# A two-block network on one core: the order of work around the first attention, and the row maxima of the second

## What is computed

```python
# first block
s = jnp.einsum('bqhd,bkhd->bhqk', qb, k) * scale
s = s + cqb[..., :, None] - c_bhs[..., None, :]
s = jnp.where(causal, s, -jnp.inf)
p = jax.nn.softmax(s, axis=-1)                      # 8 heads of 64, 1024 keys
sgu = spatial_gating(jax.nn.gelu(z), ...)           # layer norm, 8 groups of 128x128
merged = concatenate([rms_norm(attn), rms_norm(sgu)])
x = x + merged @ w_out
...
# second block: 16 query heads, window of 128 plus 256 context keys, and a sink
logits = concatenate([s_lat, s_ctx, sink])
p = jax.nn.softmax(logits)
```

## Time and profile before

| | us |
|---|---|
| median of 3 runs (2851.93 to 2857.03) | 2852.97 |
| the profiled execution | 2850.02 |
| its span, first to last instruction | 2848.2 |
| PE busy | 2735.5 (96% of the span) |
| DVE busy | 2040.7 (72%) |
| ACT busy | 1312.3 (46%) |

### The profile page before, as it was taken

How to read it: one execution, slowest core, us unless ns; L and a number is a source line. 1 busy time by engine, 2 the same in 40 slices (tenths; PEclk the granted TensorE clock), 3 DMA queues, 4 the chain that set the end, 5 groups by cost and what they waited for, 6 DMA issues and landing times.

```text
span 2848.2 us, 35308 instructions
## 1 busy us (share of the span) xinstructions
PE 2735.5 (96%) x13692; PEld 2189.3 (77%) x13692; DVE 2040.7 (72%) x2919; ACT 1312.3 (46%) x2019; POOL 555.6 (20%) x499
## 2 busy tenths in 40 slices
PE   7999999999999999999999999999999399999996
PEld 6777778788778888988888876666788288888885
DVE  5344444888885688887867656766765689999997
ACT  4344533433323455433222345444323277777775
POOL 0011011655555110511111121111100300010000
PEclk9999999999999999999999999999999699999998
DMA  4210113344661998233222261111664599999996
GB/s 147 54 45 30 45 50 133 99 141 138 188 181 57 350 296 238 81 93 115 89 72 77 104 197 33 41 42 38 207 215 156 222 352 398 396 395 397 396 395 236
DMA packets 270618, 494.12 MB, mean 173 GB/s; under 512 B 30124, under 2 KB 141892, under 8 KB 269940
## 3 DMA queue, kind: packets, MB, share of 16 engines
q1 hardware_dynamic: 240864, 396.40, 40.0%
q0 software_dynamic: 29440, 95.43, 10.4%
q10 hardware_dynamic: 148, 0.04, 0.0%
HBM read 424.60 MB, written 67.21 MB: 173 GB/s over the span
## 4 chain that ended last, share of the span: by engine, by line
PE 88%; DVE 7%; ACT 2%; issue 2%; DMA 1%; POOL 1%; POOLq 0%; DVEq 0%; SPq 0%; ACTq 0%
PE PS L132 82%; PE PS L135 6%; DVE m L141 3%; ACT m L138 1%; DVE m L150 1%; DVE m L147 1%; DMA m<-h_scratch 1%; POOL m L141 1%; DVE m L183 0%; DVE m L186 0%; DVE m L180 0%; ACT L138 0%; DVE m L156 0%; DVE small L144 0%; DMA m<-in_x_dram 0%
## 5 line engine op out<-in xcount | busy, mean ns | idle before, releaser
L132 PE MATMUL PS<-m,m 128*128 128x512 f32 (+6 forms) x11818 | 2532.7, 388 | 22.5 <-DVE m L141 9.8
L132 PEld LDWEIGHTS PS<-m,m 128*128 128x128 f32 (+2 forms) x11818 | 1985.8, 184 | 501.5 <-issue 94.3
L138 ACT ACTIVATE m<-m 128x512 fp32r<-128x512 f32 (+5 forms) x893 | 811.5, 929 | 898.7 <-PE PS L132 386.7
L141 DVE TENSOR_TENSOR m<-m,m 128x512 fp32r<-128x512 f32 (+5 forms) x920 | 1024.7, 1143 | 219.3 <-ACT m L138 197.2
L138 ACT ACTIVATE m<-PS 128x512 f32<-128x512 f32 (+3 forms) x481 | 268.3, 581 | 500.6 <-PE PS L135 310.5
L141 DVE TENSOR_TENSOR m<-PS,m 128x512 f32<-128x512 f32 (+1 forms) x456 | 300.6, 685 | 191.7 <-PE PS L132 143.8
L141 POOL TENSOR_TENSOR m<-m,m 128x512 f32<-128x512 f32 (+4 forms) x176 | 273.2, 1557 | 604.1 <-DVE m L141 259.9
L135 PE MATMUL PS<-ident,m 128*128 128x128 f32 x1650 | 231.4, 279 | 67.2 <-DVE m L156 36.0
L135 PEld LDWEIGHTS PS<-ident,m 128*128 128x128 f32 x1650 | 192.3, 143 | 114.9 <-DVE m L156 36.3
L150 DVE CUSTOM_DVE_ANT_0 m<-PS,m 128x640 f32<-128x640 f32 (+4 forms) x192 | 146.3, 774 | 97.1 <-PE PS L132 97.1
L138 ACT ACTIVATE m<-m,small 128x640 f32<-128x640 f32 (+4 forms) x200 | 157.4, 790 | 73.4 <-DVE small L150 66.7
(11 more groups left out here) (88 smaller groups left out, 483.6 us busy)
## 6 DMA issues: line engine op xcount, KB each, us to landing
m<-in_w_exp_gate_dram SPq DMA_DIRECT2D x64, 1024.0 KB, 8.7
m<-in_w_exp_up_dram SPq DMA_DIRECT2D x64, 1024.0 KB, 9.0
m<-in_w_exp_down_dram SPq DMA_DIRECT2D x64, 1024.0 KB, 8.6
m<-in_w_mod_dram SPq DMA_DIRECT2D x48, 512.0 KB, 3.8
m<-in_w_gate_up_dram SPq DMA_DIRECT2D x44, 512.0 KB, 6.4
m<-in_w_in_dram SPq DMA_DIRECT2D x21, 1024.0 KB, 5.2
m<-in_w_in_dram SPq DMA_DIRECT2D x25, 512.0 KB, 5.2
x_scratch<-m POOLq DMA_DIRECT2D x24, 512.0 KB, 3.9
```

Of the source, the lines that this page charges most:

```text
L132: return Unsent() if self.e is None else self.e.matmul(o, l, r, start=first, stop=last, **k)
L138: return Unsent() if self.e is None else self.e.activation(o, i, fn, **k)
L141: return Unsent() if self.e is None else self.e.tensor_tensor(o, a, b, op)
```

## The change

It has four parts, and no transfer of SyncE or GpSimd is added or taken away.

1. **First attention.** In step 0 the first filler call stands ahead of the scores of step 1; in all other steps it stands behind the first two transposes, so that the twelve filler matmuls form one run.
2. **z.** The rounding of `W_Z + 2` moves ahead of the squares of the tiles that `o1_scale(7)` writes (ACT) and ahead of `o1_scale(7)` (DVE). ACT takes the four GELUs out of PSUM first, then all eight high parts of `at8`, then `W_Z + 3`, then the four GELUs in SBUF.
3. **Merge.** The transposes of `zu` go in pairs between groups of `w_out`; the rounding of `W_O + 1` moves ahead of the squares.
4. **Second attention.** The reduction works on negated scores, takes the minimum and starts from the negated sink, so that `nms` comes out of it; the small instruction goes (128 of them), and the exponential has scale -1. The copy of bank 7 (16 of them) moves from DVE to ACT, behind the exponentials of the step, the last one behind `sink_exp(15)`.

```diff
@@ attn1_pe
+                if s == 0:
+                    between1(pe, 0, 0)
                 if s + 1 < NS1:
                     qk1(pe, s + 1)
                 if s:
                     values1(pe, s - 1)
-                between1(pe, s, 0)
                 for c in range(min(n, 2)):
                     turn1(pe, s, c)
+                if s:
+                    between1(pe, s, 0)
                 between1(pe, s, 2)
@@ z_act
+                if h:
+                    w_high(act, W_Z + 2)
...
-            for i in range(4):
-                act.wait_ge(*q1_out(16 + i))
-                act.activation(zv[:, i, :], zv[:, i, :], ACT.Gelu)...
-            w_high(act, W_Z + 2)
...
+            w_high(act, W_Z + 3)
+            for i in range(4):
+                act.wait_ge(*q1_out(16 + i))
+                act.activation(zv[:, i, :], zv[:, i, :], ACT.Gelu)...
@@ z_dve
+            w_low(dve, W_Z + 2)
             o1_scale(dve, 7)
@@ merge_pe
+            for i in range(5):
+                wo_group(0, 0, i)
+            pe.kept = range(6)
+            turn_zu(0)
+            turn_zu(1)
+            wo_group(0, 0, 5)
+            turn_zu(2)
+            turn_zu(3)
+            wo_group(0, 1, 0)
+            turn_zu(4)
+            turn_zu(5)
+            wo_group(0, 1, 1)
+            turn_zu(6)
+            turn_zu(7)
@@ max2
-                                         scale=0.125, scalar=-3.0e38, op0=ALU.add, op1=ALU.max, accum_out=m1)...
-                dve.wait_ge("s2_max", s, a)
-                dve.tensor_scalar(nms[:, i % 2, h:h + 1], m1, sinkr[:, h:h + 1], -1.0, ALU.max, ALU.mult)...
+                                         scale=-0.125, scalar=nsink[:, h:h + 1], op0=ALU.add, op1=ALU.min,
+                                         accum_out=nms[:, i % 2, h:h + 1])...
@@ mix_act
+                if s > 4 and s % 4 == 1:
+                    o2_take(act, s // 4 - 1)
                 for h, k in y_parts(s):
                     y_high(act, h, k)
             sink_exp(act, 15)
+            o2_take(act, 15)
@@ o2_normed
-            dve.wait_ge("o2_acc", g)
-            dve.tensor_copy(on[g % 2], PS[:, 7, :]).then_inc(*dve.did("o2_taken", g))
```

More of the change, by code:

```diff
@@ L1057, in z_act @@
                 act.activation(ma[0][:, :, tile128(i)], turned("at_turned", i), ACT.Copy).then_inc(*act.did("at_high", i))
-                if i == 1:
-                    w_high(act, W_Z + 3)
+            w_high(act, W_Z + 3)
+            for i in range(4):
+                act.wait_ge(*q1_out(16 + i))
+                act.activation(zv[:, i, :], zv[:, i, :], ACT.Gelu).then_inc(*act.did("z_out", 0, i))
             root_of(act, zr, "ln")
@@ L1091, in z_dve @@
                                   ALU.subtract).then_inc(*dve.did("at_low", i))
-                if i == 1:
-                    w_low(dve, W_Z + 3)
-            for i in range(4, 8):
+            w_low(dve, W_Z + 3)
+            for i in (4, 5, 6, 7, 0, 1, 2, 3):
                 z_norm(dve, i)
@@ L1128, in merge_sp @@
                 w_load(sp, n)
-        WO_ORDER = [(0, 0, 6), (0, 0, 7)] + [(0, 1, i) for i in range(NT)] + [
+        WO_ORDER = [(0, 1, 2), (0, 0, 6), (0, 0, 7)] + [(0, 1, i) for i in range(3, NT)] + [
             (1, kg, i) for i0 in (0, 4) for kg in range(2) for i in range(i0, i0 + 4)]
@@ L1145, in merge_pe, with wo_group, turn_zu @@
                 pe.matmul(PS[:, b, :], wsT[:, g, :], zv[:, :, g * 64:(g + 1) * 64], True, True).then_inc(*pe.did("sg_acc", g))
[L1146 to L1150, removed]
+            def wo_group(c, kg, i):
+                pe.wait_ge(*(("zu_low", i) if kg else ("at_low", i)))
+                tok_group(pe, W_O + 2 * c + kg, i, 4 * kg, 4, 8, mlhs, "wo_acc", (c, kg, i), ("x1_half", c, i))
+            def turn_zu(i):
                 pe.wait_ge(*zu_scaled(i))
                 turn4(pe, zu[:, i, :], 0, 4, "zu_turned", (i,), ("zu_low", i))
+            for i in range(5):
[12 more added lines that the diff above has]
+            turn_zu(7)
             pe.kept = ()
             for c, kg, i in WO_ORDER:
-                pe.wait_ge(*(("zu_low", i) if kg else ("at_low", i)))
-                tok_group(pe, W_O + 2 * c + kg, i, 4 * kg, 4, 8, mlhs, "wo_acc", (c, kg, i), ("x1_half", c, i))
+                wo_group(c, kg, i)
                 if (c, kg, i) == (1, 0, 7):
@@ L1164, in merge_act @@
         def merge_act(act):
+            w_high(act, W_O + 1)
             act.wait_ge("sg_out", 7)
@@ L1206, in merge_dve @@
                                          ALU.add, ALU.mult).then_inc(*dve.did("sg_out", g))
+            w_low(dve, W_O + 1)
             for h in range(2):
@@ L1214, in merge_dve @@
                 dve.tensor_scalar(zu[:, i, :], zu[:, i, :], rs8[:, i:i + 1], None, ALU.mult).then_inc(*dve.did("zu_scaled_v", i))
-            w_low(dve, W_O + 1)
             for i in range(NT):
@@ L3127, in exp2 @@
             h = heads[a]
-            act.wait_ge("s2_shift", s, a)
+            act.wait_ge("s2_max", s, a)
             v = S2[s % 3][a][:, 0:128 * len(keys2(i))]
-            act.activation(v, v, ACT.Exp, bias=nms[:, i % 2, h:h + 1], accum_out=rsum[:, i % 2, h:h + 1]).then_inc(
+            act.activation(v, v, ACT.Exp, bias=nms[:, i % 2, h:h + 1], scale=-1.0, accum_out=rsum[:, i % 2, h:h + 1]).then_inc(
                 *act.did("s2_exp", s, a))
@@ L3136, in sink_exp, with o2_take @@
             act.activation(esk[:, hs], esk[:, hs], ACT.Exp).then_inc(*act.did("sink_exp", g))
+        def o2_take(act, g):
+            act.wait_ge("o2_acc", g)
+            if g >= 2:
+                act.wait_ge("o2_out", g - 2)
+            act.activation(on[g % 2], PS[:, 7, :], ACT.Copy).then_inc(*act.did("o2_taken", g))
         def mix_act(act):
```

16 lines of the change are left out of this document (4 added, 12 removed).

## The result

The changed kernel takes 2833.54 us (median of 4 runs, 2832.55 to 2836.8), the kernel before 2852.45 beside it (4 runs). The ratio is 0.9938 [0.9926, 0.995]: faster by 18.9 us between the medians, by the interval 0.5 to 0.7%. The profiled execution took 2833.19, which is 16.8 less than the profiled execution of before (2850.02).

What follows compares the result with a forecast made beforehand. TensorE, busy 96% of the span, was taken as the bound; gains of 2.6 + 1.6 + 2.7 + 5.8 - 0.4 = 12.3 us took 2852.97 to a forecast of 2840.7 us, range 2836.5 to 2846.

Steps and rivals of the forecast that it cites:

- the start: First attention, up to the scores of step 2: filler shortens the 2.57 us wait and the clock holds; gain 2.6 us.
- z: Stage z: GELUs that free PSUM banks come first, so the second half starts at 341.35 instead of 344.04; gain 2.7 us.
- Merge: Transposes of `zu`: twelve matmuls between pairs cover the trip through ACT and DVE; gain 5.8 us.
- rival c: Merge: the load of `x` is late by 3 us more, a 1.3 us wait, time 2842.0 us; chance 0.06.
- The start of the second attention: Dropping one small instruction a step for three steps shortens the path of the reductions; gain about 1.2 us.
- its end: End of the second attention: bank 7's copy stands ahead of ACT's high parts and delays the projection; loss 1.6 us.
- rival d: Second attention: the 16 moved copies lie on the path, costing 9.4 us, time 2850.1 us; chance 0.04.
- rival (e): Second attention: the reduction starting from memory takes longer, harmless below 1.3 us more each, slower kernel from 1.4; chance 0.03.
- TensorE does not wait for DVE in a group, so 15 groups give nothing: Second attention's groups: work taken off DVE gains 0, and a group keeps its 21.33 us.
- 0.05 us a step, 1.6 us in all: First attention's other 31 steps: one run of twelve fillers changes the seams, gaining 0.05 us a step, 1.6 in all.
- Rival (b): First attention: by the rule that changing tiling mode drains TensorE, 31 steps gain nothing, time 2842.3 us; chance 0.10.
- 5.0 for the seam: First attention's 31 steps, upper bound: if two values records take only 0.1 us, 0.16 us a step, 5.0 in all.

Runs made afterwards that it cites:

- e6: The kernel before with only the copy of bank 7 in the second attention moved from DVE to ACT: 2854.67 us, ratio 1.0007.
- e7: The changed kernel with the last of the 16 copies of bank 7 kept on DVE: 2832.54 us, ratio 0.9934.
- e5: The kernel before with only the second attention's new reduction (minima of negated scores, no small instruction): 2847.85 us, ratio 0.9991.
- e15: The changed kernel with the second attention put back as in the kernel before: 2835.31 us, ratio 0.9947.
- e2: The kernel before with only the first attention's new order of filler matmuls: 2846.05 us, ratio 0.9984.
- e1: The kernel before, unchanged, timed against itself: 2849.71 against 2851.94 us, ratio 0.9999.
- e9: The changed kernel with DVE's `o1_scale(7)` put ahead of the low parts of `W_Z + 2` in z: 2834.79 us, ratio 0.9937.
- e3: The kernel before with only the new order of rounding, high parts and GELUs in z: 2847.94 us, ratio 0.9984.
- e13: The changed kernel with merge put back as in the kernel before: 2845.76 us, ratio 0.9975.
- e4: The kernel before with only the transposes of `zu` in merge set in pairs between groups of `w_out`: 2844.72 us, ratio 0.9978.
- e8: The changed kernel with the first filler call in step 0 of the first attention put back behind the transposes: 2838.55 us, ratio 0.9951.
- e11: The kernel before with four more matmuls in the first group of merge, so that its gaps lie later: 2854.24 us, ratio 1.0009.
- e12: The kernel before with eight more matmuls in the first group of merge, so that its gaps lie later: 2855.4 us, ratio 1.0009.

## Why the prediction was right, and where it failed

**The steps that held.** The release of the first scores stayed where it was, the clock held behind the shorter wait, and the start gave 2.4 where 2.6 was forecast. z gave 2.7 as forecast, with a wait of 1.0 us where 0.9 was expected. Merge gave 5.5 where 5.8 was forecast, and the load of `x` was not late (rival c). The start of the second attention gave 1.0 (forecast 1.2), its end cost 1.6 (forecast 1.6), and e6 and e7 put that down to the last copy of bank 7 standing ahead of ACT's high parts. The moved copies cost nothing in the groups (rival d). The reduction with its start value from memory takes 880 ns instead of 818, 0.06 more, far from the 1.3 from which rival (e) would have begun. Because of it VectorE is 27.6 us less busy and not 38. ScalarE is not 10 us busier; a group of the copy alone (e6) has it busy for 10.59 us, one of the reduction alone (e5) for 9.62, and why the latter is less than the 10.10 of before was not looked into.

**The step that failed.** It reads: "TensorE does not wait for DVE in a group, so 15 groups give nothing". They gave 2.4 us, 0.2 in each of twelve. The row of PE was read as if a matmul's end were observed; the stall of 0.37 instead of 0.17 us between the third chunk of transposes and the sums is visible only as idle time of the weight loads, ended by DVE's copy. e5 alone brings the gain, e6 alone does not, e15 loses it again.

**The term that was too small.** "0.05 us a step, 1.6 us in all" came out as 2.9. Two short waits of before (0.24 us at 273.6 and 0.22 at 306.3), which the merged run covers, are 0.45 of it; the rest is 2.4 over 31 steps, 0.08 a step, nearer to the 0.09 of the prediction for the merged run by itself than to the 0.05 that it took. That the merged run is what gives the 2.4 is an inference: e2 measures the whole reordering. Rival (b), which gave the steps nothing by the drain rule of the Trainium skill (TensorEngine Tiling, Key Properties), falls as a forecast of the time, since e2 alone gives 2.9 in the steps: it seems that one seam between fillers and transposes less is worth something, whatever the seam behind the values costs. What that seam costs in each order was not measured by itself.

**What stood between profile and median.** The sum was made against one execution and subtracted from a median, on the silent ground that the stalls of before cost the same every time. They do not. The profiled execution of before had paid for the fall of the clock at the first attention (1.6 us), which six of nine traces paid, and for the one at 2296 us (1.6), which eight of seventeen paid, but not for one in merge, which five of nine traces paid with 1.6 to 3.1 us, 1.3 us on average over the nine. So the 16.8 us between the two profiles hold 2.5 of scatter in favour of the changed kernel: the 1.6 at 2296, and the 0.85 before the first attention (e1 and e9 have none of that, e3 has more).

The medians' gain is larger than the profiles' all the same, by 2.1 us. The falls in merge, which the new order never had in eight traces, can be a part of it. How large a part no run shows, and other terms pull the other way: the fall at the first attention is worth less on average than in the profile of before, and the loss near 2068, which is 0.6 in the changed kernel's trace, is 1.2 to 6.2 in its seven relatives. e13 and e4 (the old merge is worth 12 and 7 us by the medians, 5.5 by its gaps) point to merge, but they also contain what happened near 2068 us. The medians of four runs may themselves be off by two us, as e1's is, and the interval of the ratio, 0.9926 to 0.995, stands for a gain of 14.3 to 21.1 us, in which 16.8 lies. So the 2.1 need no cause at all, and whether they have one stays open.

In sum, of the 6.6 us that the forecast missed, 2.4 are the groups, 1.3 the steps, 0.85 the scatter ahead of the first attention, 2.1 the gap between profile and median; the terms of the other stages were 0.7 too high together, and 0.7 came from behind the second attention, where the luck of the clock at 2296 gave 1.6. Even the two mis-sized terms put right, 12.3 + 3.7 = 16.0, give 2837.0 and not 2833.5. The range was drawn too narrow as well: its low end is said to be 16.5 us of gain, but its own terms (5.0 for the seam, half of the way from 2.6 to 3.3 for the start) add up to 16.05, and its high end (1.8, 1.3 and 1.1 lost) to 2844.9 and not 2846. It allowed for nothing in the groups and nothing for scatter.

## What to carry to other kernels

A busy TensorE row doesn't rule out short waits: look at the idle time of the weight loads, by form, and at who ended it, before a stage is put down as worth nothing. A gap of TensorE is worth more than its length where the granted clock may fall behind it, and one profile tells only whether it fell that time; several traces of nearly the same kernel show how often. The same holds for stages that a change does not touch: before a difference of two profiles is credited to a change, compare the granted clock there too. A mend that is worth one or two us can be shown stage by stage in a trace long before the run times can show it, but look also where a later stage, paced by its transfers, takes the gain back.

## What the runs showed of the hardware

- The same gaps of TensorE bring a fall of the granted clock to 0.50 in some executions and not in others. At the start of the first attention a wait of 2.57 us, always with the same release, cost 12.6 us for the stage in before, e1, e5, e6, e8 and e11, and 10.98 in e3, e4 and e12. Counted from the clock's first fall in the same trace, the wait ended after 88.1 to 88.9 us in the six and after 89.4 to 89.7 in the three. The Trainium skill (TensorE: Matmul & The Clock Gate, What's actually happening) says that the window in which activity is watched runs freely and does not start with the kernel; the traces agree with it in that the same stage falls or not by its distance from an earlier change of the clock.
- Gaps of 0.9 to 1.4 us suffice for a fall, where four follow each other with eight transposes between them; a single one of 1.0 us, as in z and at the start of the changed kernel, brought it in none of fourteen cases (six in z, eight at the start).
- One of 1.4 us with eight transposes and one of 0.54 behind it, at 2293.83 in before, brought a fall in eight of seventeen traces, for 1.6 us. One of 2.57 to 2.61 us, in the old z, brought it in nine of nine; one of 2.40 (e9) and one of 2.75 (e7) near 2068 did not.
- The reduction of VectorE that starts from a value in memory and takes a minimum needs 880 ns for 128x640 and 747 for 128x512, where the one with a constant and a maximum takes 818 and 684 (means of 96 and 32 in each trace). Its accumulator read stays at 82 to 83 ns.
